# One decoder step with a recurrent branch: side work of the recurrence moved singly into the gaps of its chain, and the sample tokens' own turn dissolved

## The reference, cut to what matters

```python
def step(s, inp):
    r_t, w_t, k_t, v_t, a_t, b_t = inp
    sa = jnp.einsum('nhvk,nhk->nhv', s, a_t)
    s = s * w_t[:, :, None, :] + sa[..., None] * b_t[:, :, None, :] + v_t[..., None] * k_t[:, :, None, :]
    return s, jnp.einsum('nhvk,nhk->nhv', s, r_t)
```

## Time and profile before

| what | value |
|---|---|
| median of three runs | 3591.2 us (3584.91 to 3594.64) |
| the profiled execution's own time | 3586.24 us |
| its span, first to last instruction | 3584.2 us |
| mean granted TensorE clock | 0.915 |
| TensorE, VectorE, ScalarE, GpSimd busy, share of the span | 86%, 32%, 27%, 9% |
| recurrent stage, first to last unit's start | 746.9 to 2000.6 us |

### The profile page before, as it was taken

How to read it: one execution, slowest core, us unless ns; L and a number is a source line. 1 busy time by engine, 2 the same in 40 slices (tenths; PEclk the granted TensorE clock), 3 DMA queues, 4 the chain that set the end, 5 groups by cost and what they waited for, 6 DMA issues and landing times. The chain is left out here.

```text
span 3584.2 us, 61851 instructions
## 1 busy us (share of the span) xinstructions
PE 3065.1 (86%) x26838; PEld 2404.0 (67%) x26838; DVE 1150.7 (32%) x2539; ACT 958.2 (27%) x1805; POOL 314.5 (9%) x294
## 2 busy tenths in 40 slices
PE   6887888787878888878887699998899999999887
PEld 4666677555555555555555466667799999999776
DVE  1111113055566655656555401110311111111132
ACT  1111111154444443434344200000312222212222
POOL 0000000000000000000000000001111112111110
PEclk8898886799999898999998699999999999999998
DMA  3213022100000000000000011102011111111101
GB/s 125 77 53 111 8 76 91 36 21 2 27 8 21 14 15 20 9 26 3 27 2 9 17 47 38 38 19 95 28 43 41 41 41 41 47 41 41 38 30 63
DMA packets 56317, 137.01 MB, mean 38 GB/s; under 512 B 4880, under 2 KB 36880, under 8 KB 51248
## 3 DMA queue, kind: packets, MB, share of 16 engines
q1 hardware_dynamic: 52224, 113.94, 9.2%
q10 hardware_dynamic: 3888, 20.05, 1.6%
HBM read 117.44 MB, written 16.54 MB: 37 GB/s over the span
## 5 line engine op out<-in xcount | busy, mean ns | idle before, releaser
L1447 PE MATMUL psum<-hT,rkv_w 128*64 128x256 f32 (+1 forms) x3072 | 463.0, 423 | 11.3 <-DMA rkv_w<-in_w_pair 10.0
L1447 PEld LDWEIGHTS psum<-hT,rkv_w 128*64 128x64 f32 x3072 | 208.9, 146 | 140.8 <-issue 62.4
L130 PE MATMUL psum<-hT,merge_w 128*128 128x352 f32 x768 | 231.4, 461 | 12.1 <-DMA merge_w<-in_w_mix 12.1
L1705 POOL TENSOR_TENSOR ff_w_low<-ff_raw,ff_w_high 128x1024 fp32r<-128x1024 f32 x64 | 157.2, 2456 | 677.6 <-ACT ff_w_high L1700 677.6
L130 PEld LDWEIGHTS psum<-hT,merge_w 128*128 128x128 f32 x768 | 146.6, 191 | 94.8 <-issue 14.3
L153 PE MATMUL psum<-ff_high,ff_w_high 128*128 128x352 f32 x768 | 172.8, 334 | 38.8 <-DVE ff_low L2004 38.8
L2007 DVE TENSOR_TENSOR rwkv_out<-rwkv_out,psum 128x1056 f32<-128x1056 f32 x64 | 80.3, 1254 | 320.8 <-PE psum L153 320.8
L153 PE MATMUL psum<-h_high,ff_w_high 128*128 128x352 f32 x768 | 167.6, 326 | 13.1 <-DVE h_low L227 12.7
L153 PE MATMUL psum<-ff_low,ff_w_high 128*128 128x352 f32 x768 | 170.3, 331 | 0.0
L153 PE MATMUL psum<-ff_high,ff_w_low 128*128 128x352 f32 x768 | 169.9, 329 | 0.0
L153 PE MATMUL psum<-h_low,ff_w_high 128*128 128x352 f32 x768 | 166.2, 325 | 0.0
(11 more groups left out here) (298 smaller groups left out, 5247.1 us busy)
## 6 DMA issues: line engine op xcount, KB each, us to landing
ff_raw<-in_w_ff SPq DMA_DIRECT2D x64, 512.0 KB, 3.4
merge_w<-in_w_mix SPq DMA_DIRECT2D x8, 1664.0 KB, 6.9
rkv_w<-in_w_pair SPq DMA_DIRECT2D x24, 512.0 KB, 4.1
rwkv_out<-in_kc ACTq DMA_DIRECT2D x4, 2048.0 KB, 13.2
ple_w<-in_w_ple SPq DMA_DIRECT2D x8, 640.0 KB, 3.9
x_in<-in_xT SPq DMA_DIRECT2D x2, 2112.0 KB, 10.8
rwkv_out<-in_xT ACTq DMA_DIRECT2D x1, 4224.0 KB, 13.8
out_yT<-y SPq DMA_DIRECT2D x8, 528.0 KB, 3.1
```

What stands on the lines that cost most here:

```text
L130: last = nc.tensor.matmul(acc[:, n, 0:TT], w[:, k, :], x[:, k, n * TT:(n + 1) * TT], start=k == 0, stop=k == kt - 1)
L1447: mm = nc.tensor.matmul(ahead[half[a], 0:width(v)], w3[:, k, n * P + a * C:n * P + a * C + C], hT[:, k, cols(v)], start=k == 0, stop=k == ...
L1705: return nc.gpsimd.tensor_tensor(parts[1][:, s, :], raw[:, s, 0:KT * P], parts[0][:, s, :].bitcast(F32), ALU.subtract)
```

## The change

It rewrites `rwkv_pairs` and nothing else. There are four parts.

1. **Side work placed singly.** On VectorE, one side instruction stands between two instructions of the chain, where before there were up to five in one gap; `mask_lower`, `mask_mixed`, `normed` are split in two; the first masks of the inverse (`Gs`, `X`) come first in the unit, ahead of `mask_rb` and the mix of k; `nmax` and the mixes of r and v move one level earlier or later; `kmod` no longer stands before the chain. `ksum` is issued one level earlier on TensorE and does not wait for the norm's logarithm any more (`bonus` does), and ScalarE's order follows.
2. **Three instructions of each unit go from VectorE to GpSimd**: `before` (pp), `kmod` (km), `bb` (av).
3. **Fill** is 4, 2, 2, 2, 1, 3 steps behind the six levels and 10 steps in the chain, mostly in twos behind the outputs `y`; the key rows and value rows of the inverse (`BK`, `zv` to token-major) follow the fill of their level.
4. **The sample turn is gone.** The sample tokens have tiles of their own, and PSUM columns in bank 2 that the prompt's groups leave free in the chain. Their grams, masks and two levels stand in the chain of the third group, their rows, `rhs`, `u`, update and outputs in the chain of the fourth. `rhs` is now 16 matmuls of 64 columns, each token against its own state, so that nothing has to be selected; the update is 16 of 64 columns, for which GpSimd spreads the keys (`sample_blocks`, 128 x 1024); one more transfer per pair brings the states a second time (`S0`). The next unit's grams stay in the chain of the fourth group.

```diff
-FILL = {"rhs": (3, 1, 1, 1), "u": (1, 1, 2, 2), "rhs last": (3, 0, 0, 0), "u last": (1, 0, 0, 0)}
+FILL_INVERSE = (4, 2, 2, 2, 1, 3)
+FILL_CHAIN = ((0, 0, 2), (0, 0, 2), (2, 0, 2), (0, 2, 0))
...
+                def sample_blocks(j):
+
+                    act_s.wait(pool, "kb", j)
+                    pe_s.wait(pool, "s", j - 1)
+                    pool_s.done("kx", nc.gpsimd.tensor_tensor(samp_KX[:, :, :, :], samp_KB[:, None, :, :].to_broadcast([P, DB, 2, C]), tok8[:, :, None, None].to_broadcast([P, DB, 2, C]), ALU.mult))
...
-                    vec_p.wait(act, "before", v)
+                    pool_v.wait(act, "before", v)
                     act_p.wait(act, "sig_a", v)
                     act_p.done("t1", nc.scalar.activation(wide(sg[v % 3], v), wide(av[v % 3], v), ACT.Identity, scale=col("k_a", j), bias=ka1[:, j:j + 1]))
...
+                def sample_rhs(j):
+
+                    act_s.wait(pe, "v1", j)
+                    vec_s.wait(pe, "mr1", j)
+                    pe.wait_ge(s0_in, 32 * j + 32)
+                    for b in range(DB):
+                        for h in range(2):
+                            last = nc.tensor.matmul(samp_RH[half[h], 0, :], samp_A[h][:, b * C:b * C + C], SVs[:, h, b, :], start=b == 0, stop=b == DB - 1)
+                    pe_s.done("rhs", last)
...
                         pe_q.done(f"u{c}", heads(UU, own, XT, rhs, other, c))
-                        for _ in range(GRAM_AT[2 * c + 1]):
-                            next(next_grams, None)
-                        fill(FILL["u last" if last else "u"][c])
-                        if c == 1 and valid(v):
+                        if last and c == 2:
+                            sample_update(j)
+                        if c < 2:
+                            next_gram()
+                        if third and c == 0:
+                            sample_gram(u, 0)
+                        if last and c == 0:
+                            sample_rows(u)
+                        if c == 2 and valid(v):
                             bonus_sum(v)
+                        fill(FILL_CHAIN[c][1])
...
-                    if last:
-                        samples(u, fill)
-                        fill(3 * KT)
-                        if valid(n):
-                            vec_s.wait(pe, "s1", j)
-                            for _ in grams(pe_g, n, range(QC), BK, H[n % 2], vec_h, pool_q):
-                                pass
...
+                        if third and c == 1:
+                            sample_straight(j)
+                        if third and c == 2:
+                            sample_level(j)
+                        if last and c == 1:
+                            sample_rhs(j)
+                        if last and c == 2:
+                            sample_state(j)
+                        fill(FILL_CHAIN[c][2])
```

More of the change, by code:

```diff
@@ L1078, in unit @@
                         part_values(v)
-                    pe_s.wait(act, "y", u // QUADS - 1)
-                    keys(act_q, pe_q, u, slice(0, QC))
+                    keys(u)
                     if valid(p):
@@ L1350, in unit @@
                     j, q = where(u)
-                    last = q == QUADS - 1
-                    pe_q.wait(vec, f"y{QC - 1}", p)
-                    mask_rb(vec_q, RB, every, gram, over)
-                    if valid(v):
-                        lerp(v, "k")
-                    def between(i):
-                        if i == 0 and valid(n):
-                            receptance(n)
+                    third, last = q == QUADS - 2, q == QUADS - 1
+                    def between(i):
+                        if i == 0:
+                            if q == 0 and valid(p):
+                                sample_decay(p)
+                            if valid(v):
+                                lerp(v, "k")
+                            if valid(n):
+                                receptance(n)
@@ L1378, in unit @@
-                    if valid(v):
-                        key_mod(v)
-                    chain(u, 0)
+                            if third:
+                                sample_operands(n)
+                    doubling(u, between)
+                    chain_rhs(u, 0)
                     if valid(v):
                         bonus_product(v)
-                    chain(u, 1)
-                    if last:
-                        mask_lower(vec_s, pe_s, j, samp_LT, 0, gram_s, one)
-                    else:
-                        mask_lower(vec_h, pe_g, n, LT, every, gram, over)
+                    chain_update(u, 0)
@@ L1389, in unit @@
                         bonus_values(v)
-                    chain(u, 2)
-                    if last:
-                        mask_mixed(vec_s, samp_H, 0, gram_s, one)
-                        mask_rb(vec_s, samp_RB, 0, gram_s, one)
-                    else:
-                        mask_mixed(vec_h, H[n % 2], every, gram, over)
-                    if valid(v):
-                        key_unit(v)
-                    if valid(p):
-                        normed(p)
-                    chain(u, 3)
+                    chain_rhs(u, 3)
@@ L1426, in _ @@
                         removal(0)
-                mask_lower(vec_h, pe_g, 0, LT, every, gram, over)
-                mask_mixed(vec_h, H[0], every, gram, over)
+                for h in range(2):
+                    mask_lower(0, h)
+                for h in range(2):
+                    mask_mixed(0, h)
                 for u in range(UNITS):
                     unit(u)
+                sample_decay(UNITS - 1)
                 normed(UNITS - 1)
+                biased(UNITS - 1)
                 gated(UNITS - 1)
@@ new lines, in sample_rows @@
+                def sample_rows(u):
+                    j = u // QUADS
+                    vec_q.wait(pe, f"xt{LEVELS - 1}", u)
+                    vec_s.wait(pe, "xt1", j)
+                    for h in range(2):
+                        for part in range(2):
+                            last = nc.tensor.matmul(samp_TK[half[part], h, :], samp_BK[:, 0, h + part, :], ident[:, half[h]], start=True, stop=True)
+                    pe_s.done("tk", last)
+                    for h in range(2):
+                        last = nc.tensor.matmul(samp_VT[half[1 - h], :], zv[u % 3][:, QT:QT + C], ident[:, half[h]], start=True, stop=True)
+                    pe_s.done("vt", last)
@@ L1592, in fill, with next_gram @@
                             next(product_ahead, None)
+                    def next_gram():
+                        for _ in range(2):
+                            next(next_grams, None)
                     def between(i):
@@ L1620, in unit @@
                         pe_q.done(f"rhs{c}", mm)
-                        for _ in range(GRAM_AT[2 * c]):
-                            next(next_grams, None)
-                        fill(FILL["rhs last" if last else "rhs"][c])
+                        if c < 2:
+                            next_gram()
+                        fill(FILL_CHAIN[c][0])
+                        if third and c == 3:
+                            sample_inverse(j)
                         if c == 3 and valid(p):
@@ L1637, in unit @@
                         pe_q.done(f"s{c}", mm)
+                        if third and c == 0:
+                            sample_gram(u, 1)
+                        if last and c == 3:
+                            sample_output(j)
                         for h in range(2):
@@ L1688, in _ @@
                             next(product_ahead, None)
-                for _ in grams(pe_g, 0, range(QC), BK, H[0], vec_h, pool_q):
+                for _ in grams(0):
                     pass
```

511 lines of the change are left out of this document (295 added, 216 removed).

## The result

The changed kernel takes **3305.8 us** (median of 4 runs, 3305.2 to 3309.6) against 3590.1 for the kernel before (4 runs, 3584.9 to 3594.6). The ratio is **0.921, 95% interval 0.919 to 0.923**. The forecast was 3376, range 3310 to 3450. The direction was right. The saving was 284 us where the sum said 210, so the time lies just under the low end of the range.

What follows compares the result with a forecast made beforehand. TensorE's queue and its waits bound the stage. Per full pair 21.8 + 3.7 + 3.5 - 1.2 = 27.8, six make 166.8; with 23 (first) and about 20 (last), 210 off 3586.2 gives 3376 us, range 3310 to 3450.

Steps and rivals of the forecast that it cites:

- the four waits in it: TensorE's waits for VectorE's `rhs` copies, ScalarE's norm logarithm, the new state and first mask `X`: 140.4 us, 5.85 per unit.
- The gaps and the fill: Recurrent units: the four TensorE waits mostly go and single fill steps fall, saving 5.45 us per unit, 21.8 per pair.
- The 0.9 per unit "that stays": Waits remaining on TensorE: some 0.3 us behind `ksum` and its maximum, 0.1 to 0.2 in each chunk.
- 0.3 per unit, 1.2 per pair: Loss in us from VectorE's mixes and `normed` running beside GpSimd's three moved instructions, half of them on the path.
- The sample turn: Fourth group: 12.7 us of turn removed, 6.1 of products put back, 2.9 of new waits; net gain 3.7 per pair.
- must be done in any case: Eight fill steps (3.6 us) and the next grams (1.16), excluded from what dissolving the 17.5 us turn saves.
- 6.1 + 2.9 = 9.0 per pair: Sample work in third and fourth groups: 6.1 us put back into TensorE's queue, 2.9 us of new waits.
- The clock: Recurrent stage mostly stays at 2.4 GHz once turn and long waits go: 3.5 us per pair, bounds 0 and 7.0.
- The lock: Each of three GpSimd instructions holds VectorE up by its whole 0.92 us: 98 us more, 3474; chance 0.13.
- The gaps refill: Chain gaps: half the 5.85 us stays and samples' waits are 5 more per pair, 104 us, 3480; chance 0.13.
- km late: `kmod` on GpSimd delays the chain's product reading km; slower overall, 3610 at 7.3 us late beyond the slack; chance 0.04.
- All goes: Recurrent stage: no wait stays, 7.0 of clock, no new waits; up to 39 us per pair, 3290 at best; chance 0.06.

Runs made afterwards that it cites:

- the shift alone: Kernel before without any sample work, eight fill steps and the next unit's grams and masks put behind the chain in every fourth group: 3459.5 us, ratio 0.965.

## Why the prediction was right in kind and short in size

**What bounds it: right.** TensorE's queue and the four waits in it were the cause. Each but the order of the first masks brought a loss when it was put back alone.

**The gaps and the fill: right, a little small.** The sum took 5.45 us per unit, 166 in all with the shorter last pair. Bunching is worth 3.05 per unit (its row said 56.1 us for 24 units, 2.34; the run also bunched one instruction more, held up the samples' masks, and lowered the clock, and how much is each wasn't separated). The logarithm is worth 1.35 in full pairs, as its row said. The fill is worth 1.24 there: 0.50 of busy time, which is the 0.5 that the sum had for single steps, and 0.75 of waits. The first masks brought nothing by their new place. Their 0.91 per unit is covered by the four fill steps. The 0.9 per unit "that stays" was 1.0 with the samples' own waits in it: 25 us of listed waits in 24 units.

**GpSimd: wrong in sign.** The step that failed is "0.3 per unit, 1.2 per pair" as a loss, 9.6 us in the sum. The runs show a gain of 0.67 per unit, 21.5 us. I had costed only what GpSimd does to VectorE's mixes, and nothing for three instructions that leave VectorE's queue, though the whole argument of the earlier trace rows was that such instructions in that queue are what TensorE waits for. This is 31 us. By itself it would not have taken the time out of the range; the terms below did that with it. The runs of the kernel before that stand beside these experiments have 3593.9, by which the saving is 288 and the sum missed 78: 38 in the placing (194.2 against 166 - 9.6), of which this is the most, and 40 in the samples and the clock, next.

**The sample turn: its own length right, its surroundings not.** The turn alone was put at 12.7 us, and the comparison of the fourth groups with the shift alone (36.4 to 39.7 us, mean 38.3) and with the turn (50.5 to 51.8, mean 51.4) gives about 13. Two terms around it were mis-sized. The eight fill steps and the next grams "must be done in any case" and were costed as equal inside and outside the chain; outside they cost 2.0 per pair more, 15.8 us, over half of it slower matmuls. And the products and waits put back were 6.1 + 2.9 = 9.0 per pair, where 7.0 were measured, 16 us in all; 0.9 per pair of this is the outputs, 1.03 instead of 1.94. With these and some 8 us that no run explains, the samples and the clock brought 93.9 us where the sum had 8 x 3.7 + 3.6 + 21 = 54.

**The clock: right as far as it was tested.** The term was 3.5 per pair, 21 us, and the idle products alone won 21.7 in the kernel before, 19.9 of it in the six full pairs. How much of the change's own gain is clock can't be read apart from the turn's: its time at the lower level ahead of the last pair fell further than with the idle products (from 157.0 us to 6.0 instead of 54.6), so 21 is likelier too little than too much. At half a microsecond each, the 151 us are worth 75 at most, by estimate.

**The rivals.** (1) *The lock* did not come about as a loss, since the move gained 21.5 us. But its mechanism is real, and my reading of the earlier trace rows against it was wrong. Where GpSimd comes first, VectorE's instruction ends only after GpSimd's (1.79 against 0.48, above). The 0.44 of the earlier trace rows was the same thing: L1290's two instructions in the kernel before end at 992.93 us, again 0.29 after the end of the GpSimd instruction of the earlier trace rows at 992.64. It lost only 0.44 because the second of them had begun 0.36 into GpSimd's 0.92, and what was left to wait for was short. Where VectorE comes first, it keeps its time and GpSimd's is the longer. VectorE's L1290 in the kernel before; then in the changed one the mix of r, GpSimd's `before` beside it and `kmod` with no such neighbour, and GpSimd's `bb` alone and beside `normed`:

```profile
991.55 1.38 DVE L1290 SCALAR_TENSOR_TENSOR H<-kkn,pp 64x256 f32<-64x256 f32 x2
...
983.76 0.46 DVE L1267 SCALAR_TENSOR_TENSOR zr<-raw_r,vec_sb,zr 128x256 f32<-128x256 f32 x1
...
983.92 0.89 POOL L945 TENSOR_TENSOR pp<-cs,sg 128x256 f32<-128x256 f32 x1 [2.99 <-DVE cs L1275]
985.52 0.73 POOL L952 TENSOR_TENSOR km<-zk,sg 128x256 f32<-128x256 f32 x1 [0.71 <-ACT sg L1046]
...
959.66 0.73 POOL L958 TENSOR_TENSOR av<-kkn,av 128x256 f32<-128x256 f32 x1 [6.21 <-DVE kkn L1297]
...
994.91 0.90 POOL L958 TENSOR_TENSOR av<-kkn,av 128x256 f32<-128x256 f32 x1
```

The Trainium skill, page "SBUF — State Buffer", section "Who interferes with whom", says this of a VectorE instruction with two SBUF inputs and a GpSimd one that reads SBUF: they shut each other out for a whole instruction, and whichever comes second waits. The rows agree in kind: VectorE as the second ended 0.28 us after GpSimd, and GpSimd as the second took 0.17 more (0.90 against 0.73). What an instruction lost here was 1.31 us at most (1.79 less 0.48), since it came 0.39 after the start of GpSimd's 1.90. It was cheap because it reached a wait of TensorE in one place per pair only, and because ScalarE was as late there, as the run with the spread moved shows. (2) *The gaps refill* did not happen: listed waits of 1.0 us per unit, not 2.9. (3) *km late* did not: `kmod` ends at 986.25 us, 13.5 into its unit (I had 13.8), some 4.4 ahead of the chain's start at 990.66. (4) *All goes*, given 0.06, was the nearest, though waits and new products did stay: 38.3 us per pair (165.7 less 127.4), where it had "up to 39".

**My own two numbers did not agree.** The sum gave 165.7 - 27.8 = 137.9 us per pair, while the part on what would show it named units of 30 to 31, 34 and 35 to 36 us, some 131. The first subtracts waits from an old pair, the second names the new units outright. The chip gave 31.00, 30.12, 32.79 and 33.45, which is 127.4. Seven microseconds per pair between two ways of one forecast are some 50 us over the stage, and they should have widened the range downward.

## What to carry to other kernels

When a serial chain runs through several engines, cost an instruction by the queue that it stands in. Here, taking three out of the queue that TensorE waits for was a gain, though they take longer on the new engine and the two engines disturb each other. Fill work was cheapest inside the chain's waits, where it also kept the clock up. Forecast such a change in two ways, by the waits that go and by laying out one new unit, and let the range hold both. Before removing a late wait, look at what else feeds the same instruction, since the next queue may be just as late.

## What was not expected of the hardware

- GpSimd's spread of 1024 columns took 1.90 us, where I had doubled the 1.28 of 512 to 2.6. The 256 columns took 0.73 with no VectorE neighbour and 0.88 to 0.92 with one.
- Where a VectorE instruction with two SBUF inputs and a GpSimd one overlapped, the one that came second paid: 1.31 us for VectorE (1.79 less 0.48), 0.17 for GpSimd (`bb`, 0.90 less 0.73).
- Nine idle products per group with a turn and five in the others made the kernel before 21.7 us faster, with TensorE's time at 1.2 GHz falling from 249.2 to 116.1 us. In the changed kernel, with its short waits, the clock stayed at 2.4 GHz by itself for 925 us.
